# Stick-breaking attention in the first stage: queries on the partitions, and sums over later keys as reversed scans

## What is computed

```python
def stick_breaking_attention(q, k, v):
    ...
        mask = key_pos[None, :] < q_pos[:, None]
        z = jnp.einsum('bhqd,bhkd->bhqk', q_blk, kh).astype(jnp.float32) * scale
        log_beta = jax.nn.log_sigmoid(z)
        log_1mb = jnp.where(mask, log_beta - z, 0.0)
        suffix = lax.cumsum(log_1mb, axis=3, reverse=True) - log_1mb
        attn = jnp.where(mask, jnp.exp(log_beta + suffix), 0.0)
        return jnp.einsum('bhqk,bhkd->bhqd', attn.astype(v.dtype), vh)

...
        q = head_rmsnorm(q.reshape(b_, s_, ATT_HEADS, HEAD_DIM), q_norm_g[l])
        k = head_rmsnorm(k.reshape(b_, s_, ATT_HEADS, HEAD_DIM), k_norm_g[l])
        y_b = stick_breaking_attention(q, k, v)

        mix = jax.nn.sigmoid(ga) * y_a + jax.nn.sigmoid(gb) * y_b
        x = x + gt1 * (mix @ w_out[l])
```

## Time and profile before

| what | us |
|---|---|
| median of 3 runs | 1697.77 (1697.17 to 1698.28) |
| the profiled execution, its own time | 1698.91 |
| its span on the core | 1697.1 |
| TensorE busy | 1649.6 (97%) |
| VectorE, ScalarE, GpSimd busy | 982.3, 801.4, 789.7 |
| first pass with attention (head 1) to the units of w_out | about 70 to 439 |

### The profile page before, as it was taken

The page is one execution under the profiler, slowest core; times in us unless marked ns, Lnnn a source line. Parts: engine busy times, 40 slices in busy tenths (PEclk is TensorE's granted clock), DMA queues, the critical chain, the costliest instruction groups (busy, mean ns, idle before and its releaser), DMA issues.

```text
span 1697.1 us, 19723 instructions
## 1 busy us (share of the span) xinstructions
PE 1649.6 (97%) x7340; PEld 1345.2 (79%) x7340; DVE 982.3 (58%) x1170; ACT 801.4 (47%) x1005; POOL 789.7 (47%) x577
## 2 busy tenths in 40 slices
PE   3999999999999999999999999999999999999997
PEld 2778887877878888888887888888877888888885
DVE  6676787777647818616633767566436554155541
ACT  2565565666544425423442333677544444244442
POOL 2244444543545455545563554455573342543525
PEclk7999999999999999999999999999999999999999
DMA  9333333242223332332222332211232121331212
GB/s 369 124 124 119 130 111 122 91 136 88 97 84 104 95 99 89 98 132 92 100 91 65 112 95 71 72 42 60 72 98 77 50 100 50 100 99 52 98 50 75
DMA packets 46462, 166.89 MB, mean 98 GB/s; under 512 B 5152, under 2 KB 5280, under 8 KB 45856
## 3 DMA queue, kind: packets, MB, share of 16 engines
q1 hardware_dynamic: 46368, 165.63, 29.1%
HBM read 163.52 MB, written 2.10 MB: 98 GB/s over the span
## 4 chain that ended last, share of the span: by engine, by line
PE 95%; DVE 2%; ACT 1%; DMA 1%; issue 0%; POOL 0%; SPq 0%; POOLq 0%; DVEq 0%; ACTq 0%
PE lin L651 17%; PE lin L653 17%; PE lin L652 17%; PE big L652 7%; PE big L651 7%; PE big L653 7%; DVE scr L1585 1%; PE big L757 1%; PE m_o L778 1%; PE big L768 1%; PE big L770 1%; PE big L1067 1%; PE big L1065 1%; PE big L1066 1%; DMA scr<-ada 1%; PE m_a L956 0%
## 5 line engine op out<-in xcount | busy, mean ns | idle before, releaser
L617 POOL TENSOR_TENSOR w_lo<-raw,w_hi 128x512 fp32r<-128x512 f32 x200 | 287.0, 1435 | 648.1 <-ACT w_hi L1104 648.0
L651 PE MATMUL lin<-h_hi,w_hi 128*128 128x512 f32 x936 | 367.7, 393 | 1.9 <-POOL w_lo L620 1.7
L653 PE MATMUL lin<-h_hi,w_lo 128*128 128x512 f32 x936 | 364.7, 390 | 0.0
L652 PE MATMUL lin<-h_lo,w_hi 128*128 128x512 f32 x936 | 364.4, 389 | 0.0
L620 POOL TENSOR_TENSOR w_lo<-raw,w_hi 128x512 fp32r<-128x512 f32 x209 | 301.4, 1442 | 14.3 <-ACT w_hi L1104 14.3
L1104 ACT ACTIVATE w_hi<-raw 128x1024 fp32r<-128x1024 f32 (+1 forms) x209 | 217.6, 1041 | 160.6 <-PE m_b L669 50.3
L651 PEld LDWEIGHTS lin<-h_hi,w_hi 128*128 128x128 f32 x936 | 175.8, 188 | 39.0 <-POOL w_lo L620 2.4
L653 PEld LDWEIGHTS lin<-h_hi,w_lo 128*128 128x128 f32 x936 | 175.7, 188 | 37.0
L652 PEld LDWEIGHTS lin<-h_lo,w_hi 128*128 128x128 f32 x936 | 175.8, 188 | 36.2 <-issue 0.5
L617 POOL TENSOR_TENSOR qk_hl<-raw,qk_hl 128x512 fp32r<-128x512 f32 x43 | 59.7, 1388 | 145.4 <-ACT qk_hl L1104 145.4
L651 PE MATMUL lin<-y_hi,w_hi 128*128 128x512 f32 x260 | 101.6, 391 | 0.0
(11 more groups left out here) (498 smaller groups left out, 3434.1 us busy)
## 6 DMA issues: line engine op xcount, KB each, us to landing
raw<-weights SPq DMA_DIRECT2D x245, 512.0 KB, 3.6
slab<-ada SPq DMA_DIRECT2D x32, 512.0 KB, 4.4
scr<-ada SPq DMA_DIRECT2D x16, 512.0 KB, 6.3
raw<-weights SPq DMA_DIRECT2D x10, 256.0 KB, 2.7
x<-x_t SPq DMA_DIRECT2D x2, 1024.0 KB, 6.1
out_t<-scr SPq DMA_DIRECT2D x8, 256.0 KB, 2.6
raw<-weights SPq DMA_DIRECT2D x4, 448.0 KB, 3.3
rgw<-rg_w SPq DMA_DIRECT2D x1, 1024.0 KB, 7.4
```

The lines of the kernel that those rows point to most:

```text
L617: nc.gpsimd.tensor_tensor(lo[:, 0:4 * P], raw[:, s, 0:4 * P], hi[:, 0:4 * P].bitcast(F32), ALU.subtract).then_inc(w_half, 1)
L651: nc.tensor.matmul(psum_of(n), wh, hi(k), start=(k == 0), stop=False)
L652: nc.tensor.matmul(psum_of(n), wh, lo(k), start=False, stop=False)
L653: last = nc.tensor.matmul(psum_of(n), wl, hi(k), start=False, stop=(k == nk - 1))
```

## The change

The scores are made with the queries on the partitions and the keys along the columns. The sum over later keys then runs along a row, and VectorE makes it as a scan from right to left, one for each block row (512, 384, 256 and 128 columns); TensorE's `suffixes` goes, and with it the split into `lm_hi` and `lm_lo`. VectorE's `exponents` does all in one go ahead of the exponential, the masks of the diagonal blocks included: a factor 0 or 1 ahead of the scans (`later`) and an addition of -30000 behind them (`bar`). Behind the exponential TensorE turns the ten blocks of weights back by transposes into `big` (`weights_turned`), behind unit yr, and VectorE copies them to SBUF (`turned_weights`) in three copies, where it masked the products before. In the last head the exponential moves ahead of gb on ScalarE. Some semaphores are merged (`x2_loaded`, `inv_loaded`, `abs_ready`, `ckv_copied`, `pad_set`), and the constant `sel_r` shrinks to `ones_r`.

```diff
             def scores(g):
 
+                for b in range(TB):
+                    i = TB - 1 - b
+                    last = nc.tensor.matmul(big_f[:, COL[i]:COL[i] + KW[i]], A(S1["q"], g)[:, b * P:(b + 1) * P],
+                                            A(S1["k"], g)[:, 0:KW[i]], start=True, stop=True)
+                last.then_inc(z_done, 1)
+
+            def weights_turned(g):
+
+                pe.wait_ge(att_exp, g + 1)
+                for of_bank in ((0,), (1, 3), (2,)):
+                    for j in of_bank:
+                        for b in range(j, TB):
+                            to, of = COL[j] + (b - j) * P, COL[TB - 1 - b] + j * P
+                            last = nc.tensor.transpose(big_f[:, to:to + P], att_a[:, of:of + P], c_("ident"))
+                    last.then_inc(att_turned, 1)
...
-            def suffixes():
-
-                for j in range(TB):
-                    for i in range(j, TB):
-                        o = COL[j] + (i - j) * P
-                        sel = sel_r[:, 0 if i == j else 1]
-                        nc.tensor.matmul(big_f[:, o:o + KW[i]], sel, lm_hi[:, COL[i]:COL[i] + KW[i]],
-                                         start=(i == j), stop=False)
-                        last = nc.tensor.matmul(big_f[:, o:o + KW[i]], sel, lm_lo[:, COL[i]:COL[i] + KW[i]],
-                                                start=False, stop=(i == TB - 1))
-                last.then_inc(suffix_done, 1)
...
-                    pe.wait_ge(lm_done, g + 1)
-                    suffixes()
                 if h == 0:
                     head_square(2, m_b[:])
                 elif h < HEADS:
...
                 if g >= 0:
                     unit("yr", g, H, L)
+                    weights_turned(g)
...
-            def shifted_logs():
...
+            def exponents(g):
+
+                dve.wait_ge(z_done, g + 1)
+                dve.wait_ge(ln_done, g + 1)
+                v.scalar_tensor_tensor(out=att_a, in0=z, scalar=0.0, in1=att_a, op0=MX,
+                                       op1=AD).then_inc(dve_order, 1)
+                dve.wait_ge(dve_order, counted(dve_order))
+                for o in own(att_a):
+                    v.tensor_tensor(o, o, c_("later").unsqueeze(1).broadcast_to([P, 2, P]), M).then_inc(dve_order, 1)
                     dve.wait_ge(dve_order, counted(dve_order))
+                for i in range(TB):
+                    rows = slice(COL[i], COL[i] + KW[i])
+                    shares = att_a[:, rows][:, ::-1]
+                    v.tensor_tensor_scan(att_b[:, rows][:, ::-1], shares, shares, 0.0, AD, MX).then_inc(dve_order, 1)
+                    dve.wait_ge(dve_order, counted(dve_order))
+                v.tensor_tensor(att_a, z, att_b, SU).then_inc(dve_order, 1)
+                dve.wait_ge(dve_order, counted(dve_order))
+                for o, signal in zip(own(att_a), (dve_order, att_t)):
+                    v.tensor_tensor(o, o, c_("bar").unsqueeze(1).broadcast_to([P, 2, P]), AD).then_inc(signal, 1)
+                    dve.wait_ge(signal, counted(signal))
+
+            def turned_weights(g):
+
+                for i, w in enumerate((T, T, 2 * P)):
+                    dve.wait_ge(att_turned, 3 * g + i + 1)
+                    v.tensor_copy(att_b[:, i * T:i * T + w], big[:, i, 0:w]).then_inc(att_done, 1)
+                    dve.wait_ge(att_done, counted(att_done))
```

More of the change, by code:

```diff
@@ L45 @@
 _at = 0
-for _name, _n in (("ident", P), ("later_ones", 2 * P), ("ones", P), ("mask", P), ("diff", T + 3 * P),
+for _name, _n in (("ident", P), ("later", P), ("ones", P), ("bar", P), ("diff", T + 3 * P),
                   ("freq_a", 1), ("freq_r", 1)):
@@ L692, in head_square @@
                 pe.wait_ge(sq_low, i)
-                nc.tensor.matmul(out, sel_r[:, 1], sq_hi[(i - 1) % 2], start=True, stop=False)
-                nc.tensor.matmul(out, sel_r[:, 1], sq_lo[(i - 1) % 2], start=False, stop=True)\
+                nc.tensor.matmul(out, ones_r[:], sq_hi[(i - 1) % 2], start=True, stop=False)
+                nc.tensor.matmul(out, ones_r[:], sq_lo[(i - 1) % 2], start=False, stop=True)\
                     .then_inc(square_used, 1)
@@ L854, in _ @@
             nc.tensor.matmul(m_a[:], rgw[:, 8 + g], A(S1["xr"], g), start=True, stop=True).then_inc(gates_done, 1)
-            pe.wait_ge(lm_done, HEADS)
-            suffixes()
+            weights_turned(g)
             for m in range(3):
@@ L1294, in _ @@
             act.wait_ge(tanh_done, counted(tanh_done))
+            act.wait_ge(att_t, HEADS)
+            nc.scalar.activation(att_a, att_a, ACT.Exp).then_inc(att_exp, 1)
+            act.wait_ge(att_exp, counted(att_exp))
             i = at("gb", g)
@@ L1304, in _ @@
             act.wait_ge(root_done, counted(root_done))
-            exp_and_log()
-            act.wait_ge(att_t, HEADS)
-            nc.scalar.activation(att_a, att_a, ACT.Exp).then_inc(att_exp, 1)
-            act.wait_ge(att_exp, counted(att_exp))
             for m in range(8):
@@ L1672, in _, with own @@
             z = big_f[:, 0:1280]
[L1674 to L1688 removed]
+            def own(of):
+                blocks = of.rearrange("p (a c) -> p a c", c=P)
+                return blocks[:, 3:7:3], blocks[:, 7:10:2]
@@ L1699, in convolve @@
                     dve.wait_ge(signal, counted(signal))
-            def mask_products():
-                for j in range(TB):
-                    o = att_a[:, COL[j]:COL[j] + P]
-                    v.tensor_tensor(o, o, c_("mask"), M).then_inc(att_done, 1)
-                    dve.wait_ge(att_done, counted(att_done))
             def decay(g):
@@ L1762, in _ @@
                 if g >= 0:
-                    dve.wait_ge(z_done, g + 1)
-                    dve.wait_ge(ln_done, g + 1)
-                    shifted_logs()
+                    exponents(g)
                 square_low(2 * h + 2)
@@ L1790, in _ @@
                 if g >= 0:
-                    dve.wait_ge(att_exp, g + 1)
-                    mask_products()
+                    turned_weights(g)
                     decay(g)
@@ L1801, in _ @@
             g = HEADS - 1
-            dve.wait_ge(z_done, HEADS)
-            dve.wait_ge(ln_done, HEADS)
-            shifted_logs()
+            exponents(g)
             decay(g)
             accumulate(NADA - 1)
-            dve.wait_ge(suffix_done, HEADS)
-            v.tensor_tensor(att_a, att_a, z, AD).then_inc(att_t, 1)
-            dve.wait_ge(att_t, counted(att_t))
-            dve.wait_ge(att_exp, HEADS)
-            mask_products()
+            turned_weights(g)
             recur(g)
@@ L2214, in constants @@
     put("ident", p == f)
-    put("later_ones", np.concatenate([p > f, np.ones((P, P), bool)], axis=1))
+    put("later", p > f)
     put("ones", 1.0)
-    put("mask", p < f)
+    put("bar", np.where(p > f, 0.0, -30000.0))
     put("diff", np.arange(T + 3 * P)[None, :] - 3 * P - p)
```

69 lines of the change are left out of this document (20 added, 49 removed).

## The result

| | kernel before | changed kernel |
|---|---|---|
| median, us | 1697.96 (1697.17 to 1698.28) | 1725.58 (1725.09 to 1726.73) |
| profiled execution, us | 1698.91 | 1725.09 |
| its span on the core, us | 1697.1 | 1723.3 |
| mean granted clock | 0.989 | 0.978 |
| ratio | 1 | 1.0163, 95% interval 1.0151 to 1.0176 |

The changed kernel is 1.6% slower. The sign is as forecast, but 1725.6 lies 16 us over the forecast and beyond the range (1693 to 1722).

A forecast was written before the change was run, and what follows sets the result against it. TensorE was taken as the bound (95% of the chain), 2.5 us behind VectorE's low half in head 3. 4 x 2.35 + 3 x 0.6 + 0.5 = 11.7 us on the median 1697.8 gave 1709.5; range 1693 to 1722, 82%.

The forecast's parts named there:

- The ledger of `exponents`: VectorE beside GpSimd in head 3: masks and scans alternate with four GpSimd instructions, so TensorE waits 4.1 us at `head_square`.
- What a head pays without the clock: Wait and transposes against the removed `suffixes`: +2.35 us in odd heads, +0.6 us in heads 2, 4 and 6.
- Head 1 was counted as an odd one: Head 1 has more GpSimd work there and paid 0.7 us already; it was priced at +2.35 us.
- The ten transposes: Added to TensorE in each head, ahead of the four of V: 0.9 to 1.1 us, taken as 1.0.
- The last head: At its turn, the transposes end at 439.5 against 439.04 before: +0.5 us.
- Nothing given back, cover of the exponential and the copies: After `head_square`: `att_exp` comes some 0.9 us early, `ga` and `gb` (11 us) cover 1.8 us of copies, nothing is regained.
- The clock: Rival at 25%: the granted clock falls in TensorE's new waits of 4.1 us, giving 1720, or 1713 in one or two heads.
- In all four heads: The falling clock's full case: a loss behind the 4.1 us waits of all odd heads, +11 us, 1720.
- Dense matmuls stand ahead of them, unlike there: Argument against a clock fall in the new 4.1 us waits, unlike the earlier 3.3 us wait, where 2.7 us were lost.
- The scans do meet GpSimd: Forecast's assumption in `exponents`; the rival (12%) had scans reading the same columns once, leaving GpSimd alone: about -3 us, 1694.5.
- reversed ones run at the forward rate: Forecast's assumption for scans; the rival (6%) had reversed scans at half that rate, +3.3 us in seven heads: 1733.
- TensorE's work does not decide: Answers a rival (12%): `exponents` and square finish in time, TensorE never waits in odd heads, 14 us gained: 1684.

The follow-up runs named there:

- fill: Changed kernel with idle matmuls of 512 columns put into TensorE's new waits (16 in odd heads, 9 in even ones, 10 in head 1): 1711.0 us.
- parts 2 and 3: Changed kernel with idle matmuls filling some waits or shifting them, 1714.5 to 1726.5 us; kernel before with low half of square made seven or ten times, 1722.1 and 1742.5.
- pool_narrow: Changed kernel with GpSimd's first-stage subtractions cut from 512 columns to 16, leaving out most low parts of the weights: 1682.0 us.
- fill_half: Changed kernel with idle matmuls filling about half of each new TensorE wait (8 in odd heads, 4 in even ones, 5 in head 1): 1714.5 us.
- psum_mask_only: Changed kernel with the masks put into the scores by TensorE, while the scans still read SBUF twice: 1691.8 us.

## Why the prediction missed

Point by point, by its own steps.

**The ledger of `exponents`: right.** 12.0 us forecast, 11.84 measured, with the masks and the scans held up by the four instructions of GpSimd as it said. The waits were 3.82 to 3.84 instead of 4.1 in odd heads, and 2.15 instead of 2.4 in even ones.

**What a head pays without the clock: right but for head 1.** +2.48 in odd heads (2.35 forecast) and +0.64 in even ones (0.6). Head 1 was counted as an odd one at 2.35 and paid 1.7 (112.70 in `fill` against 111.01 before, at its first gate matmul, is 1.69 too). That is the one mis-sized term without the clock, 0.6 us too much. That the whole comes to the 11.7 us of the forecast is partly luck: what this term has too much, the others together have too little.

**The ten transposes: right.** 0.9 to 1.1 was the forecast; with nothing slow around them they stand 1.09 us apart from the next matmul, first to first (100.89 to 101.98 in head 1):

```profile
100.89 1.25 PE L761 MATMUL big<-cst,scr 128*128 128x128 f32 x10
101.98 0.60 PE L811 MATMUL m_o<-cst,scr 128*128 128x128 f32 x4
```

**The last head: right.** `att_t` came 10.15 us behind VectorE's start (10.1 forecast); without the clock +0.6 against the +0.5 forecast.

**Nothing given back, cover of the exponential and the copies: right.** There is no wait at the turn in heads 1 to 7, nor at the gates.

**The clock: this step failed.** The prediction named it as a rival, with 25%, and left it out of the sum. It took two rows of the kernel before, a fall behind 3.3 us and none behind 2.2, and read a border between them: a wait of 4.1 might bring a fall, one of 2.4 would not. Two things in that were wrong.

- *Its condition.* One wait without a fall is one draw. The very wait that it read, 2.22 us, had a fall behind it in 3 of 12 kernels. The table above has seven waits of 2.15 to 2.37 with seven falls, and three waits of 2.76 in one execution with two. So the even heads, head 1 and the turn of the last head were given no price at all.
- *Its extent.* "In all four heads" was the rival's worst case, 11 us and 1720. It was eight places, 15.2 us: 2.5 to 2.6 in each of the three odd heads, close to the 2.7 of the earlier trace rows, and 1.3 to 1.7 in the five others.

"Dense matmuls stand ahead of them, unlike there", the argument against a fall, is refuted by parts 2 and 3: dense matmuls stood ahead of the waits that fell. With a price of 2.6 and 1.5 us behind each wait the same ledger gives 11.7 + 3 x 2.6 + 5 x 1.5 = 27.0 us, 1724.8; these prices are read from the result, so the sum shows only that nothing else is missing.

**The other rivals.** The scans do meet GpSimd, and reversed ones run at the forward rate. TensorE's work does not decide, but it would at the times of `pool_narrow`, without meetings: 1685 to 1687 by what the attention gains there, where the rival said 1684. That the meetings could be taken away by changing one operand wasn't seen. The engines don't meet at semaphores alone, as the first section has it: VectorE and GpSimd also meet at operands in SBUF.

**Small slips in the working.** By its own rows, 14 matmuls in 5.8 us lose 5.8 - 14 x 0.23 = 2.6 us, not 2.7, and the case without meetings of the scans adds up to -2.8 us, 1695.0, not 1694.5. Neither changes anything.

## What to carry to other kernels

Price each new wait of TensorE between dense matmuls at its own length and, from about 2 us on, at up to 1.5 to 2.6 us more: near 2 us, where seven of seven fell at one place and 5 of 18 at others, as a chance; from 3.8 us on, where all 16 fell, in full. Read the length of a fixed run of matmuls behind it rather than the list of waits, which doesn't show the loss. A run of VectorE that reads two operands from SBUF while GpSimd does the same pays for each meeting; before an order is changed, see whether one operand can stay in PSUM, or whether TensorE can do the masks as one more product into the scores.

## What the runs showed of the hardware that was not expected

- The granted clock can fall behind a wait of 1.02 us (stretch 7.61 instead of 6.03), and stay up behind 2.76 and 3.15. Behind equal waits of 3.83 in one execution the loss was 1.6 or 2.7 us. Losses come in two sizes, 1.3 to 1.8 and 2.5 to 2.9 us. Where the clock had fallen early in the wait, less of it was left to lose: in the kernel with nine more squares heads 3 and 5 have equal waits, at a mean clock of 0.66 and 0.93, and stretches of 7.63 and 8.90 us behind them:

```profile
204.30:209.16 4.86, 0.00 (x0) 0.03 (x1) 4.62 (x8) 0.00 (x0) 0.00 (x0) 0.66 0.00 0
209.16:216.79 7.63, 7.63 (x26) 6.12 (x27) 7.38 (x8) 1.70 (x3) 0.00 (x0) 0.77 0.71 250
314.30:319.20 4.90, 0.00 (x0) 0.03 (x1) 4.66 (x8) 0.00 (x0) 0.00 (x0) 0.93 0.00 0
319.20:328.10 8.90, 8.90 (x27) 6.98 (x27) 8.62 (x9) 2.93 (x4) 0.00 (x0) 0.66 0.68 236
```

  What decides the moment of a fall stays open.
- A scan whose second operand lies in PSUM isn't held up by GpSimd (1220 ns at most for 512 columns, in 32 scans) and doesn't hold it up (1.31 us for the subtraction inside the scans). With both operands in SBUF, though they are the same columns, it is: at worst 2219 ns instead of 1220.
- Executions of kernels with waits near the edge scatter more: 1711.5 to 1717.0 in `fill_half`, where those of `psum_mask_only` lie within 1.1 us.
